# Wide passes of a routed expert layer: down projection with strided stationary weights, VectorE block transposes and quarter-row scatters

## What is computed

```
v = rms_norm(h, norm2_g)
logits = v @ router_w + router_b
top_val, top_idx = top_k(logits, 4);  gates = softmax(top_val)
for each of a token's 4 experts e (of 32):
    z = v @ w1[e] + b1[e]                       # 1024 -> 2048
    x_glu = min(z[:1024], 7);  x_lin = clip(z[1024:], -7, 7)
    act = x_glu * sigmoid(1.702 * x_glu) * (x_lin + 1)
    y += gate * (act @ w2[e] + b2[e])           # 1024 -> 1024
out = h + y
```

## Time and profile before

| | us |
|---|---|
| median of 3 runs | 1993.06 |
| lowest, highest | 1991.5, 1994.81 |
| the profiled execution | 1994.85 |
| its span, first to last instruction | 1993.1 |
| TensorE matmul busy | 1925.4 (97%) |
| weight loads busy | 1589.3 (80%) |
| VectorE busy | 1010.1 (51%) |
| ScalarE busy | 449.9 (23%) |
| GpSimd busy | 415.6 (21%) |
| mean granted clock of TensorE | 0.992 |

### The profile page before, as it was taken

One profiled execution on the slowest core, in us unless ns is written; L12 is line 12 of the kernel. 1 busy time (PEld: TensorE's weight loads), 2 busy tenths in 40 slices (PEclk: granted clock), 3 DMA queues, 4 the chain that ended last, 5 costly groups with the idle time before them and its releaser, 6 DMA issues.

```text
span 1993.1 us, 35237 instructions
## 1 busy us (share of the span) xinstructions
PE 1925.4 (97%) x12983; PEld 1589.3 (80%) x12984; DVE 1010.1 (51%) x2627; ACT 449.9 (23%) x983; POOL 415.6 (21%) x410
## 2 busy tenths in 40 slices
PE   5999989989999999999999999999999999999996
PEld 3545545457888877888887888999999999999996
DVE  2989973354555545555554555444444444443332
ACT  3166565111111111111111111222222211211111
POOL 3111100011222222222232222222222222221211
PEclk9999999999999999999999999999999999999998
DMA  7000033538999999999999999999888899887651
GB/s 242 1 1 1 6 112 136 186 114 293 349 343 332 352 338 350 351 341 332 351 339 351 351 347 331 313 323 311 303 301 302 304 308 308 298 294 244 223 181 40
DMA packets 237153, 513.21 MB, mean 258 GB/s; under 512 B 11085, under 2 KB 15721, under 8 KB 237104
## 3 DMA queue, kind: packets, MB, share of 16 engines
q1 hardware_dynamic: 215408, 448.89, 62.6%
q0 software_dynamic: 19840, 63.23, 11.9%
q10 hardware_dynamic: 1856, 0.41, 0.1%
HBM read 479.30 MB, written 33.19 MB: 257 GB/s over the span
## 4 chain that ended last, share of the span: by engine, by line
PE 91%; DVE 4%; ACT 2%; issue 1%; DMA 1%; POOL 0%; SPq 0%; ACTq 0%; DVEq 0%; POOLq 0%
PE bank L1175 50%; PE bank L1219 12%; PE bank L1194 12%; PE bank L1392 5%; PE bank L1267 4%; DVE arena L932 2%; PE bank L1303 2%; PE bank L1314 1%; PE bank L1207 1%; PE bank L1553 1%; PE bank L1208 1%; PE bank L1342 1%; DMA arena<-in_x 1%; PE bank L1259 0%; PE bank L1366 0%
## 5 line engine op out<-in xcount | busy, mean ns | idle before, releaser
L1175 PE MATMUL bank<-arena 128*128 128x128 f32 (+5 forms) x8192 | 1000.7, 284 | 6.9 <-issue 6.1
L1175 PEld LDWEIGHTS bank<-arena 128*128 128x128 f32 x8192 | 986.5, 191 | 18.8 <-issue 17.8
L377 POOL DMA_INDIRECT arena<-token_rows,idx_q x256 | 250.1, 977 | 649.0 <-PE bank L1175 589.1
L808 DVE TENSOR_SCALAR arena<-bank,b1c 128x256 f32<-128x256 f32 x256 | 123.4, 482 | 407.2 <-PE bank L1175 407.2
L497 ACT ACTIVATE arena<-arena 128x256 f32<-128x256 f32 x256 | 106.6, 417 | 853.9 <-DVE arena L808 853.9
L1219 PE MATMUL bank<-arena 128*128 128x512 f32 x576 | 250.2, 592 | 0.0
L1194 PE MATMUL bank<-arena 128*128 128x144 f32 (+4 forms) x1792 | 246.8, 293 | 3.0 <-ACT arena L501 2.9
L1194 PEld LDWEIGHTS bank<-arena 128*128 128x128 f32 x1792 | 235.3, 190 | 6.2 <-ACT arena L501 6.2
L383 POOL DMA_INDIRECT out<-arena,idx_cur x64 | 99.4, 1553 | 535.9 <-DVE arena L865 492.1
L1219 PEld LDWEIGHTS bank<-arena 128*128 128x128 f32 x576 | 108.1, 190 | 129.1 <-issue 129.1
L932 DVE SCALAR_TENSOR_TENSOR arena<-arena,cols 128x512 f32<-128x512 f32 (+1 forms) x226 | 182.3, 807 | 12.5 <-ACT arena L592 5.5
(11 more groups left out here) (229 smaller groups left out, 1102.4 us busy)
## 6 DMA issues: line engine op xcount, KB each, us to landing
arena<-in_w SPq DMA_DIRECT2D x192, 2048.0 KB, 12.6
arena<-in_b SPq DMA_DIRECT2D x32, 512.0 KB, 12.7
arena<-in_x SPq DMA_DIRECT2D x16, 512.0 KB, 6.4
token_rows<-arena SPq DMA_DIRECT2D x8, 576.0 KB, 3.2
out<-arena SPq DMA_DIRECT2D x8, 512.0 KB, 6.0
arena<-token_rows,idx_q POOLq DMA_INDIRECT x256
arena<-in_w_in SPq DMA_DIRECT2D x2, 1536.0 KB, 13.1
arena<-in_w_in SPq DMA_DIRECT2D x1, 3072.0 KB, 19.5
```

What stands on the lines that cost most here:

```text
L377: pool.indirect_dma_start(out=gath_q[:, g, :], out_offset=None, in_=quads_d, in_offset=bass.IndirectOffsetOnAxis(ap=idx_q[:, g:g + 1], axis=0)
L808: v.tensor_scalar(g1[:, r, :], bank[r][:, 0:SLOTS], b1c[:, m:m + 1], LIMIT, ALU.add, ALU.min).then_inc(g1_ready, 1)
L1175: last = mm(bank[m % 2][:, side * SLOTS:side * SLOTS + n], w1_sb[:, k, lo:lo + P], xT[:, k, 0:n], start=k == 0, stop=k == KD - 1)
```

## The change

In wide passes the stationary side of down product d is every eighth column of w2, from column d on, in place of 128 neighbouring ones. Partition c of product d is then output feature 8c + d, and each group of 32 partitions holds one quarter of the features. `trans_y` and `take_y` are gone. ScalarE copies a product to `yT` with the bias added (a new column-wise bias tile `b2c`), VectorE transposes it in 32x32 blocks into `y_turned` (`turn_y`; four before and four after the transposes of the gathered rows), in which a partition is a token's quarter row, and ScalarE applies the gate and brings the features into order (`weigh_quads`, eight instructions). GpSimd sends eight scatters of quarter rows in pairs: the first pair when it is ready, the next three after hidden groups 0, 1 and 2 of the next pass. One semaphore `added` counts all scatters, and GpSimd waits for all that were sent at the start of each pass; VectorE's wait for them moves from m = 4 to m = 6. A narrow pass sends one scatter, without the zeros. VectorE runs `turn_y` in every pass, and in a wide pass the two gate-and-bias steps on a tile that isn't sent. Both halves of w2 wait for the whole down stage. Ahead of the first pass there are two more small products and a few small VectorE instructions.

```diff
         def load_b2(sp, e):
             sp.dma_start(b2_rows, src.to_broadcast([P, D])).then_inc(b2_in, 16)
+            sp.dma_start(b2c[:], src.rearrange("o (p d) -> (o p) d", d=KD)).then_inc(b2c_in, 16)
...
                     load_w1(sp, c, e)
+                sp.wait_ge(y_mm, q * KD)
                 for c in range(2):
-                    sp.wait_ge(y_mm, q * KD + (4 * c + 4 - KD))
                     load_w2(sp, c, e)
...
+        def add_quads(pool, groups):
+            pool.sem_inc(pool_past, 1)
+            for g in groups:
+                pool.indirect_dma_start(out=out_quads,
+                                        out_offset=bass.IndirectOffsetOnAxis(ap=idx_q_cur[:, g:g + 1], axis=0),
+                                        in_=y_quads[:, g, :], in_offset=None, compute_op=ALU.add).then_inc(added, 16)
...
             with pool.Fori(0, n_pass) as q:
+                pool.wait_ge(added, pool.snap(sent, min_val=32, max_val=32 + 128 * QMAX))
+                pool.sem_inc(landed, 1)
                 over = pool.value_load(tabI[0:1, ds(q + TQ, 1)])
                 pool.wait_ge(idx_q_ready, q + 1)
                 for i in range(4):
                     pool.wait_ge(hid_mm, q * 8 + 5 + i)
                     gather_quads(pool, (2 * i, 2 * i + 1))
-                pool.wait_ge(y_ready, q + 1)
-                for i in range(2):
-                    pool.wait_ge(added[i], q * 16 + 16)
-                pool.sem_inc(pool_past, 1)
-                add_rows(pool, 0, ytok[:, 0, :])
                 with pool.If(over < 1):
-                    add_rows(pool, 1, zeros)
+                    pool.wait_ge(y_ready, q + 1)
+                    add_rows(pool)
+                    pool.reg_add(sent, sent, 16)
                 with pool.Else():
-                    add_rows(pool, 1, ytok[:, 1, :])
+                    for i in range(4):
+                        pool.wait_ge(quads_ready, q * 4 + (i + 2))
+                        if i >= 1:
+                            pool.wait_ge(hid_mm, q * 8 + (8 + i))
+                        add_quads(pool, (2 * i, 2 * i + 1))
+                    pool.reg_add(sent, sent, 128)
...
             def take_yT(d):
+                if d == 0:
+                    a.wait_ge(b2c_in, q * 16 + 16)
+                    a.wait_ge(turned, q + 1)
                 a.wait_ge(y_mm, q8 + d + 1)
-                a.activation(yT[:, d, :], bank[2 + d % 2][:, 0:SLOTS], ACT.Copy).then_inc(yT_ev, 1)
...
+                a.activation(yT[:, d, :], bank[2 + d % 2][:, 0:SLOTS], ACT.Identity, bias=b2c[:, d:d + 1]).then_inc(yT_ev, 1)
+
+            def weigh_quads():
+                a.wait_ge(cur_ready, q + 1)
+                a.wait_ge(turned, q + 2)
+                for g in range(8):
+                    last = a.activation(y_quads[:, g, :].rearrange("p (i d) -> p d i", d=KD),
+                                        y_turned[:, g, :].rearrange("p (d i) -> p d i", d=KD), ACT.Copy,
+                                        scale=gate_q_cur[:, g:g + 1])
+                    if g % 2 == 1:
+                        last.then_inc(quads_ready, 1)
...
-                for d in range(6):
+                for d in range(KD):
                     take_yT(d)
-                take_y(0)
-                take_yT(6)
-                take_yT(7)
-                take_y(1)
+                weigh_quads()
...
+            def turn_y(d):
+                v.wait_ge(yT_ev, q8 + d + 3)
+                return v.transpose(y_turned[:, :, d * 32:(d + 1) * 32], yT[:, d, :].rearrange("p (g r) -> p g r", r=32))
+
+            v.wait_ge(quads_ready, q * 4 + 1)
+            for d in range(KD // 2):
+                turn_y(d)
             v.wait_ge(quad_in, q * 128 + 128)
...
+            for d in range(KD // 2, KD):
+                last = turn_y(d)
+            last.then_inc(turned, 1)
...
                     last = mm(bank[2 + d % 2][:, 0:n],
-                              w2_sb[:, m, d * P:(d + 1) * P], act[:, m, 0:n],
+                              w2_sb[:, m, :].rearrange("p (c d) -> p d c", d=KD)[:, d, :], act[:, m, 0:n],
                               start=m == 0, stop=m == MT - 1)
...
-            for d in range(2, 6):
+            for d in range(2, KD):
                 down(d, range(MT))
-                trans_y(d - 2)
-            down(6, range(MT))
-            down(7, range(MT))
-            for d in range(4, KD):
-                trans_y(d)
```

More of the change, by code:

```diff
@@ L54, in hybrid_block @@
     quads_d = rows_d.rearrange("s (q c) -> (s q) c", q=4)
+    out_quads = out2.rearrange("s (q c) -> (s q) c", q=4)
     with ExitStack() as ctx:
@@ L92, in hybrid_block @@
         g2_row = part(140, D)
-        ytok = part(144.5, 2, D)
+        y_quads = part(144.5, 8, D // 4)
+        y_turned = part(164.5, 8, D // 4)
+        ytok = part(172.5, D)
         zeros = part(140, D)[0:2, :]
@@ L193, in hybrid_block @@
         idx_q = sb("idx_q", [P, 8], i32)
+        idx_q_pass = sb("idx_q_pass", [P, 8], i32)
+        idx_q_cur = sb("idx_q_cur", [P, 8], i32)
+        gate_q_pass = sb("gate_q_pass", [P, 8])
+        gate_q_cur = sb("gate_q_cur", [P, 8])
+        b2c = sb("b2c", [P, KD])
         copies = sb("copies", [P, P])
@@ L247, in hybrid_block @@
         y_mm, yT_ev, yt_mm, yt_ev = sem("y_mm"), sem("yT_ev"), sem("yt_mm"), sem("yt_ev")
-        added = [sem(f"added{i}") for i in range(2)]
+        added, landed, turned, quads_ready, b2c_in = (sem(n) for n in (
+            "added", "landed", "turned", "quads_ready", "b2c_in"))
         pool_past = sem("pool_past")
@@ L518, in take_rows @@
                     a.wait_ge(cur_ready, q + 1)
-                    for i in range(2):
-                        a.wait_ge(added[i], q * 16 + 16)
-                a.activation(ytok[:, 0, b * HALF:(b + 1) * HALF], bank[4 + b][:], ACT.Copy,
+                a.activation(ytok[:, b * HALF:(b + 1) * HALF], bank[4 + b][:], ACT.Copy,
                              scale=gate_cur[:, 0:1]).then_inc(yt_ev, 1)
-                a.sem_inc(yT_ev, KD // 2)
             with a.If(over < 1):
                 sigmoids()
+                a.sem_inc(yT_ev, KD)
                 take_rows(0)
                 take_rows(1)
+                a.sem_inc(quads_ready, 4)
             with a.Else():
                 sigmoids()
-                for d in range(6):
+                a.sem_inc(yt_mm, 2)
+                a.sem_inc(yt_ev, 2)
+                for d in range(KD):
                     take_yT(d)
-                take_y(0)
-                take_yT(6)
-                take_yT(7)
-                take_y(1)
+                weigh_quads()
         @block.scalar
@@ L773, in _ @@
             a.sem_inc(yT_ev, 2)
+            a.sem_inc(quads_ready, 1)
             a.wait_ge(tab_ready, 1)
@@ L840, in dve_pass @@
                 if m == 3:
-                    v.wait_ge(spread_mm, q + 1)
+                    v.wait_ge(spread_mm, q + 2)
+                    link(v.tensor_copy(idx_q_pass[:], idx_q[:]))
                     v.tensor_scalar(idx_q[:], bank[6][:, 16:24], 4.0, quad_id[:], ALU.mult, ALU.add
                                     ).then_inc(idx_q_ready, 1)
-                if m == 4:
-                    for i in range(2):
-                        v.wait_ge(added[i], q * 16 + 16)
+                if m == 6:
+                    v.wait_ge(landed, q + 1)
                     v.tensor_copy(idx_cur[:], idx_pass[:])
+                    v.tensor_copy(idx_q_cur[:], idx_q_pass[:])
+                    v.tensor_copy(gate_q_cur[:], gate_q_pass[:])
                     link(v.tensor_copy(gate_cur[:], gate_pass[:]))
@@ L1151, in _ @@
             link(v.tensor_tensor(rank[:], rka[:], rkd[:], ALU.add))
+            v.wait_ge(spread_mm, 1)
+            v.tensor_copy(gate_q_pass[:], bank[3][:, 8:16])
+            link(v.tensor_scalar(idx_q[:], bank[3][:, 0:8], 4.0, quad_id[:], ALU.mult, ALU.add))
             for i in range(4):
@@ L1187, in down @@
                 if 0 in ms:
-                    if d % 4 == 0:
-                        pe.wait_ge(w2_in[d // 4], q16)
+                    if d == 0:
+                        for c in range(2):
+                            pe.wait_ge(w2_in[c], q16)
                     pe.wait_ge(yT_ev, q8 + d + 1)
@@ L1198, in down @@
                     last.then_inc(y_mm, 1)
-            def trans_y(d):
-                pe.wait_ge(yT_ev, q8 + d + 3)
-                if d == 0:
-                    pe.wait_ge(yt_ev, q2)
-                if d == 4:
-                    pe.wait_ge(yt_ev, q2 + 1)
-                c = (d % 4) * P
-                pe.transpose(bank[4 + d // 4][:, c:c + P], yT[:, d, 0:P], ident[:])
-                last = pe.transpose(bank[7][:, c:c + P], yT[:, d, P:], ident[:])
-                if d % 4 == 3:
-                    last.then_inc(yt_mm, 1)
             def down_rows(b, ms):
@@ L1579, in _ @@
             pe.wait_ge(tab_ready, 1)
+            pe.wait_ge(spots_ready, 1)
+            for i, src in enumerate((spots, gsel)):
```

(3 more changed lines are left out.)

47 lines of the change are left out of this document (23 added, 24 removed).

## The result

| | before | after |
|---|---|---|
| median | 1993.38 us (1991.5 to 1994.81, 4 runs) | 2161.52 us (2161.3 to 2162.28, 4 runs) |
| span of the profiled execution | 1993.1 us | 2159.6 us |
| ratio | | 1.0845, interval 1.0826 to 1.0864 |

The forecast was 1964.5 us, range 1954 to 1990. The kernel became 168 us slower and lies 197 us over the forecast: the rival of strided loads came true, and it is dearer than I had priced it (2132). The granted clock is as before, 0.99 on the mean.

The account below looks back on a forecast made before the run. TensorE was taken to bound the kernel, its hidden products being half the chain of waits. Terms -34.2 + 0.3 + 5.4 = -28.5 us took the profiled 1994.85 to 1966.3, less 1.8 for the median: 1964.5 us, range 1954 to 1990.

Parts of the forecast that it names:

- the rival of strided loads: Rival in wide down products: each weight load occupies the load path 0.223 us, unhidden; price 168 us, time 2132, chance 0.17.
- Strided stationary weights: Wide down products' weight loads with columns 8 words apart: cost bounded between 0 and 168 us, taken as 0.
- the 50 ns of slack: TensorE weight loads: ordinary ones take 190 ns, transposes' 140, so memory was said to deliver columns at least 50 ns faster.
- my upper end of 168: Wide down products: load occupancy doubles to about 0.223 us and sets the pitch, costing 1792 x 0.094 = 168 us.
- Transposes and pass ends: Wide down stages on TensorE: transposes go and idle time at pass ends closes, a gain of 34.2 us over 14 passes.
- the costs of 0 for VectorE and SP: VectorE's extra turns stay hidden under TensorE, and SP's later w2 loads land before TensorE wants them; cost 0 each.
- ScalarE: "Cost 0": Eight scaled copies after the last turn, done 4 to 6 us into the next pass, don't reach TensorE; cost 0.
- GpSimd: the times right, the cost of 0: Eight scatters, last at 16.1 us into the next pass, gathers from 24.4 to 25.9; hidden with 2 to 3 us left.
- a late xT: Rival: scatters land late, delaying gathers and xT, so TensorE waits at each wide pass; called 1980 us, chance 0.09.
- Start and end: Two more small products before the first pass, +0.3 us; unhidden scatters at the end, tail 18.0 to 23.4, +5.4 us.
- The sum: Whole kernel: -34.2 + 0.3 + 5.4 = -28.5 us, giving a median of 1964.5 us; forecast with its bounds had chance 0.70.

Follow-up runs that it names:

- Experiment 3: Changed kernel with wide-pass weight columns read at steps 1 to 16 and narrow-pass moving columns at steps 2 and 4, output meaningless; 2216.1 us, one execution.
- experiment 6: Changed kernel with ScalarE reordering w2 on the chip for contiguous loads, plus a plain copy out of the bank without the b2 bias; 1969.76 us.
- experiment 7: First four gathers moved ahead of the scatter-landing wait: 1968.17 us on experiment 1, 1968.59 us on the changed kernel with w2 reordered on the chip by ScalarE.
- experiment 1: Changed kernel with 128 neighbouring weight columns per wide down product again, so output columns are permuted; 1977.07 us, ratio to before 0.9911.
- experiments 5: experiment 1 with only four of the eight quarter-row scatters per wide pass, half of the wide passes' result missing; 1963.05 us, ratio 0.9851.

## Why the prediction was wrong, step by step

**Strided stationary weights: the step that failed.** "I take 0, by the 50 ns of slack" gave 0, measured were 435.2 less 240.7 = 194.5 us in the down stages, beyond my upper end of 168 as well. Two errors stand in it. The first is the inference: the two loads of 190 and 140 ns are both contiguous, and say nothing about a read whose columns lie apart. Experiment 3 gives the slack that there really was: a step of 2 (205 ns) fits, a step of 3 (261 ns) costs half as much again (2.77 us for 16 instructions against 1.85), a step of 4 (329 ns) twice as much. The second is the size: doubled occupancy was a guess with a round factor, 0.223 us; the runs give 0.239 to 0.242 per instruction. Its half, 0.1115, stands in no row either; with the 0.1145 of the earlier trace rows the upper end would have been 179, still short.

The rule of the Trainium skill named there (Advanced Engine Details and Errata, section SBUF Cachelines) forecast the direction and, as experiment 3 shows (205 ns at step 2, 329 at step 4), where the price is full. I had it beside a trace that didn't contradict it, and gave it 0.17. A stated rule against an inference from rows that don't show the operation should have carried at least even odds.

**Transposes and pass ends: right.** Forecast -34.2. With contiguous weights and the gathers moved, the down stages sum to 240.7 against 271.8, -31.1, and the hidden groups give about 1.3 more, since the wait at the start of a pass is gone (30.36 against 30.46 us at 136 columns): -32.4. A 136-wide stage takes 15.53 to 15.55, not 15.33. Of the difference 0.09 is ScalarE's copy with bias (experiment 6); all of it lies before the third product. The pass end closed, as reasoned: no wide pass of the changed kernel or of experiment 7 has idle time ahead of its hidden products. So the costs of 0 for VectorE and SP stood too.

**ScalarE: "Cost 0" was off, by 0.09 us a pass.** I counted the eight copies out of the way, and overlooked that the copy out of the bank, on the path before the third product, becomes Identity with a bias, 475 ns for 384. The eight scaled copies took 4.35 us in the changed kernel and hid.

**GpSimd: the times right, the cost of 0 only beside strided loads.** Scatters and gathers came when forecast, and in the changed kernel itself that cost nothing: its gathers are bunched as well, but no engine was late there (VectorE 0.20 us after TensorE). With contiguous loads it cost 8.0 us in experiment 1 (248.7 less 240.7), in seven of the 14 passes; 1.7 of them are the half clock that followed the idle time. I had looked for it in a late xT. It came at the other end: VectorE, ScalarE and GpSimd take up TensorE's work some 2 us late while gathers are issued back to back beside the last hidden group.

**Start and end.** Forecast +0.3 and +5.4. The end is +7.1: the issues as forecast, the last landing 8.9 us and not 7.3. The first wide pass began 2.8 us earlier than before (1226.40 against 1229.21), but that moment lies between 1225.6 and 1229.3 in all these runs but experiment 3, contiguous or not, and goes with the granted clock in the first half, which no edit touches: in the windows 90:130, 250:330 and 400:480 us it is 0.96, 0.94 and 0.98 before and 1.00, 0.96 and 0.98 after. By an estimate from these, 0.04 x 40 + 0.02 x 80 = 3.2 us. So it isn't the change's, and the two small products more can't be read from it.

**The sum, by spans.** By the spans the forecast was 1993.1 - 28.5 = 1964.6, and 2159.6 is 195.0 more. The stride makes 194.5, the transposes 1.8, the tail 1.7, the start -3.1: 194.9. That the start fell on this side is chance; the other terms are what the runs show.

## What to carry to other kernels

A free dimension of f32 that is read with a wide step is not free on TensorE: on the stationary side it cost time from a step of 3 words, on the moving side at 4 (3 wasn't tried), and at 2 next to nothing on either; put the permutation where time is idle (here ScalarE's copies, 117.6 us beside TensorE) and keep the loads contiguous. A trace shows the slack of an operation only for the access that it shows: where the new access is of another kind, price it from both ends and let a stated rule weigh. And when a queue gets longer work, look also at how its next work is spaced: with contiguous loads, gathers that lost their pacing cost 8.0 us, and the scatters themselves only a longer end (the down stages sum to 240.8 us with four of them and 240.7 with eight).

## What the runs showed of the hardware

- **Weight loads by step**, 128 f32 columns: 190, 205, 261, 329, 318, 335, 312 ns for 1, 2, 3, 4, 5, 8, 16 words; the pitch of instructions (from start to start) at 136 columns goes from 0.1157 us at step 1 to 0.239 at step 8. Moving side, 512 columns: 0.434, 0.450, 0.899 us for 1, 2, 4.
- **Small scatters cost GpSimd as much as large ones.** A quarter-row scatter takes 1583 ns on the mean (112 of them, L399 of the changed kernel), a full-row one of the narrow passes 1627 (18 of them), with 0.30 us between two. I had priced them alike. They landed a little sooner: 7.3 us at the median (3.7 to 8.6) against 8.3 of full rows; from the last issue to the end it was 8.9 us, where it was 12.3.
- **Late counts.** With gathers back to back beside the last hidden group, other engines went on some 2 us after TensorE's records end: 4 waits of VectorE, 2 of GpSimd and 1 of ScalarE in experiment 1 (up to 3.7 us long) have no releaser on the core. Spacing the gathers ends it (experiments 5 and 7), and so do strided loads in all wide products: the changed kernel has no such wait, though its gathers are bunched too. Experiment 3, whose first two products of each wide pass load contiguously, has them again (3 of VectorE, up to 3.8 us long, and 3 of GpSimd). So bunched gathers and contiguous loads behind the last hidden group were there each time. Whether the counts come late or TensorE's records end early, and why not in every pass, isn't settled: no run isolates it.
- **A short idle time can cost twice.** In experiment 1 TensorE ran only the last four instructions of a product between 1309.0 and 1312.6 us; within a microsecond of taking up again the granted clock fell from 1.00 to 0.50 for some 3 us, which cost 1.7 us of the stage on top of the 2.7 waited.
